# State scan of a hybrid decoder step: decays spread by DMA through DRAM, subtract and clip on ScalarE, output banks doubled

## What is computed

```python
def ssd_chunked(xs, dt, a, bm, cm, h0):
    xd = xs * dt[..., None]
    ad = dt * a
    def step(h, inp):
        xd_c, ad_c, b_c, c_c = inp
        acs = jnp.cumsum(ad_c, axis=1)
        seg = acs[:, :, None] - acs[:, None, :]
        lmat = jnp.exp(jnp.where(causal[None, :, :, None, None], seg, -jnp.inf))
        cb = jnp.einsum('blgn,bsgn->blsg', c_c, b_c)
        y_diag = jnp.einsum('blsg,blsgr,bsgrp->blgrp', cb, lmat, xd_c)
        y_off = jnp.einsum('blgn,bgrpn,blgr->blgrp', c_c, h, jnp.exp(acs))
        decay_end = jnp.exp(acs[:, -1:] - acs)
        h_new = h * jnp.exp(acs[:, -1])[..., None, None] + jnp.einsum('bsgn,bsgr,bsgrp->bgrpn', b_c, decay_end, xd_c)
        return h_new, y_diag + y_off
```

## Time and profile before

| what | value |
|---|---|
| median of 3 runs | 6118.93 us (6109.17 to 6125.71) |
| profiled execution | 6095.56 us, its span 6093.8 us |
| TensorE, VectorE, ScalarE, GpSimd busy | 4488.3, 3624.1, 1143.9, 2491.0 us |
| TensorE clock granted, mean | 0.864 |
| moved by DMA | 1467.90 MB, mean 241 GB/s |
| eight `ssd_chunk` stages | about 54 us (two) and 62 to 71 us (six) |

### The profile page before, as it was taken

One profiled execution on the slowest core, in us unless ns is written; L12 is line 12 of the kernel. 1 busy time (PEld: TensorE's weight loads), 2 busy tenths in 40 slices (PEclk: granted clock), 3 DMA queues, 4 the chain that ended last, 5 costly groups with the idle time before them and its releaser, 6 DMA issues. The chain is left out here.

```text
span 6093.8 us, 52161 instructions
## 1 busy us (share of the span) xinstructions
PE 4488.3 (74%) x16596; PEld 2712.1 (45%) x16596; DVE 3624.1 (59%) x8352; ACT 1143.9 (19%) x2862; POOL 2491.0 (41%) x2215
## 2 busy tenths in 40 slices
PE   6965982577878777469788777588777878547768
PEld 5344872453534555153444556273443566212223
DVE  4056437755656667676665767774566565854441
ACT  2022310111222111020222212111222201101111
POOL 0000010245433764436543444226433475377775
PEclk9965995788889988789898989799889989779999
DMA  3300740467565998679777976458666798599998
GB/s 128 112 17 19 260 146 0 158 232 258 180 213 183 381 336 302 205 269 373 264 234 247 390 271 227 130 181 306 206 205 202 266 394 315 187 351 409 395 377 306
DMA packets 574392, 1467.90 MB, mean 241 GB/s; under 512 B 59448, under 2 KB 250264, under 8 KB 567608
## 3 DMA queue, kind: packets, MB, share of 16 engines
q0 software_dynamic: 307200, 1115.82, 51.5%
q1 hardware_dynamic: 253960, 314.47, 15.3%
q10 hardware_dynamic: 12960, 34.26, 1.4%
HBM read 1418.60 MB, written 45.80 MB: 240 GB/s over the span
## 5 line engine op out<-in xcount | busy, mean ns | idle before, releaser
L2621 PE MATMUL bank<-vring,diag 128*128 128x512 f32 (+1 forms) x3064 | 1565.5, 649 | 474.7 <-ACT diag L2602 192.2
L2507 POOL DMA_INDIRECT uring<-in_peer_u,eidx x1024 | 1186.9, 1159 | 1227.3 <-DVE uring L2539 742.3
L2574 POOL DMA_INDIRECT vring<-in_peer_v,eidx x1024 | 1134.3, 1108 | 1336.7 <-PE bank L2621 935.1
L2539 DVE SCALAR_TENSOR_TENSOR uring<-uring,xr 128x1024 f32<-128x1024 f32 x1040 | 1263.9, 1222 | 585.2 <-DMA uring<-in_peer_u,eidx 540.0
L2621 PEld LDWEIGHTS bank<-vring,diag 128*128 128x128 f32 (+1 forms) x3064 | 572.8, 202 | 1279.7 <-issue 815.4
L634 PE MATMUL bank<-wt,xT 128*128 128x512 f32 (+3 forms) x1440 | 606.3, 580 | 90.1 <-DMA wt<-in_w_in 82.6
L2602 ACT ACTIVATE diag<-ident,wt 128x128 f32<-128x128 f32 x750 | 289.0, 398 | 1149.6 <-PE bank L2621 1034.1
L634 PEld LDWEIGHTS bank<-wt,xT 128*128 128x128 f32 (+1 forms) x1440 | 241.0, 178 | 444.1 <-issue 348.0
L2654 DVE SCALAR_TENSOR_TENSOR x_tok<-vring,wt,x_tok 128x1024 f32<-128x1024 f32 x274 | 356.7, 1302 | 90.8 <-DMA vring<-in_peer_v,eidx 76.8
L489 PE MATMUL bank<-xT,wx 128*128 128x264 f32 (+1 forms) x1536 | 371.6, 405 | 34.0 <-DMA wx<-in_w_in 33.8
L489 PEld LDWEIGHTS bank<-xT,wx 128*128 128x128 f32 x1536 | 307.7, 202 | 87.3 <-DMA wx<-in_w_in 34.1
(11 more groups left out here) (464 smaller groups left out, 5507.5 us busy)
## 6 DMA issues: line engine op xcount, KB each, us to landing
wt<-in_w_in SPq DMA_DIRECT2D x32, 2048.0 KB, 12.7
wx<-in_w_in SPq DMA_DIRECT2D x48, 1024.0 KB, 6.5
wm<-in_w_in SPq DMA_DIRECT2D x32, 1024.0 KB, 22.6
wm<-in_w_branch_a SPq DMA_DIRECT2D x32, 1024.0 KB, 15.4
wq<-in_peer_wq SPq DMA_DIRECT2D x32, 1024.0 KB, 9.0
tokm<-tout ACTq DMA_DIRECT2D x64, 256.0 KB, 4.6
s_h<-in_state_ssm SPq DMA_DIRECT2D x16, 1024.0 KB, 9.5
wm<-in_w_branch_b SPq DMA_DIRECT2D x16, 1024.0 KB, 13.4
```

What stands on the lines that cost most here:

```text
L2507: pool.indirect_dma_start(out=G.uring[:, K % UR, :], out_offset=None, in_=table, in_offset=bass.IndirectOffsetOnAxis(ap=E.tiles[q][3][:, j ...
L2539: dve.scalar_tensor_tensor(row, row, 1.0, G.xr[:, q % 2, :], ALU.mult, ALU.mult, accum_out=G.pre[:, q % 2, j:j + 1]).then_inc(G.dotted, 1)
L2574: pool.indirect_dma_start(out=G.vring[:, K % VR, :], out_offset=None, in_=table, in_offset=bass.IndirectOffsetOnAxis(ap=E.tiles[q][3][:, j ...
L2621: mm = pe.matmul(G.bank[6 + c][0:m, :], G.diag[:, R % DR, 0:m], G.vring[:, K % VR, c * BANK:(c + 1) * BANK], start=first, stop=last, skip_ ...
```

## The change

A DRAM tensor `decays` of 2x32x128 is added. SP writes `acsT` there, waits until it has landed, and reads it back four times, each time 8 rows (4 KB) broadcast to all 128 partitions, into three buffers of `eb` instead of two; the fourth waits for the first diagonal group. The spread matmuls are gone. ScalarE computes Relu(acs - spread value) for each head in place (8 instructions of 128x128 a group) and then Exp of the negative. VectorE has only the weighing, the masked product and the combine left; the masked product of the next group comes before the combine of this one. The diagonal part alternates between banks 0 and 1, the update of the state between 3 and 4, the part from the earlier state between 2 and 5, so L790 of a group waits for the combine two groups back. The copy of `acsT` comes first of the decay copies, and the mask product after them. The fractions at which expert slots are put into the order are shifted (`at`).

```diff
+EBR = 3
@@ ssd_chunk
-        eb, xdd, tmp = sb("eb", [P, 2, HPG * P]), S.xdd, S.ytmp
+        eb, xdd, tmp = sb("eb", [P, EBR, HPG * P]), S.xdd, S.ytmp
+        def at(g):
+            return 0.35 + 0.65 * max(0.0, g) / NG
@@ sync
             sp.dma_start(S.z[:], G.tokm[t * P:(t + 1) * P, 0:DI]).then_inc(sem("z"), 16)
+            sp.wait_ge(sem("acs"), 2)
+            sp.dma_start(G.decays[j], acsT[:]).then_inc(sem("kept"), 16)
+            sp.wait_ge(sem("kept"), 16)
+            for g in range(NG):
+                if g >= EBR:
+                    sp.wait_ge(sem("ydiag"), g - EBR + 1)
+                sp.dma_start(eb[:, g % EBR], G.decays[j, g * HPG:(g + 1) * HPG].rearrange("h l -> (h l)").partition_broadcast(P)
+                             ).then_inc(sem(f"spread{g % EBR}"), 16)
@@ scalar
             for g in range(NG):
-                go(0.25 + 0.75 * g / NG)
+                go(at(g - 0.8))
+                act.wait_ge(sem(f"spread{g % EBR}"), 16 * (g // EBR + 1))
+                for r in range(HPG):
+                    h = g * HPG + r
+                    e = eb[:, g % EBR, r * P:(r + 1) * P]
+                    act.activation(e, e, ACT.Relu, bias=acs[:, h:h + 1], scale=-1.0).then_inc(sem("seg"), 1)
                 act.wait_ge(sem("seg"), HPG * (g + 1))
-                act.activation(eb[:, g % 2], eb[:, g % 2], ACT.Exp).then_inc(sem("lmat"), 1)
+                act.activation(eb[:, g % EBR], eb[:, g % EBR], ACT.Exp, scale=-1.0).then_inc(sem("lmat"), 1)
@@ tensor
-            pe.wait_ge(sem("acs"), 3)
-            pe.wait_ge(sem("decays"), 3)
             pe.wait_ge(sem("xs"), 4)
-            def spread(g):
...
-            spread(0)
             for g in range(NG):
-                if g + 1 < NG:
-                    spread(g + 1)
-                go(0.25 + 0.75 * (g + 0.5) / NG)
-                if g == 0:
+                go(at(g - 0.1))
+                if g == 1:
                     pe.wait_ge(sem("cbm"), 1)
-                else:
-                    pe.wait_ge(sem("combined"), g)
-                pe.matmul(bank[5][:], cur[:, XT + NG + g, :], hT[:, g, :], start=True, stop=True)
+                    pe.wait_ge(sem("acs"), 3)
+                    pe.wait_ge(sem("decays"), 3)
+                elif g >= 2:
+                    pe.wait_ge(sem("combined"), g - 1)
+                pe.matmul(bank[(2, 5)[g % 2]][:], cur[:, XT + NG + g, :], hT[:, g, :], start=True, stop=True)
                 pe.wait_ge(sem("xdd"), g + 1)
-                pe.matmul(bank[3][:], btok[:, g, :], xdd[:, g % 2], start=True, stop=True)
+                pe.matmul(bank[3 + g % 2][:], btok[:, g, :], xdd[:, g % 2], start=True, stop=True)
+                go(at(g + 0.1))
                 pe.wait_ge(sem("mmat"), g + 1)
...
                 mm.then_inc(sem("ydiag"), 1)
-                go(0.25 + 0.75 * (g + 0.6) / NG)
+            go(0.95)
@@ vector
-            def prepare(g):
...
-                for r in range(HPG):
-                    h = g * HPG + r
-                    dve.tensor_scalar(eb[:, g % 2, r * P:(r + 1) * P], bank[r // 4][:, (r % 4) * P:(r % 4 + 1) * P],
-                                      acs[:, h:h + 1], 0.0, ALU.subtract, ALU.min).then_inc(sem("seg"), 1)
-            prepare(0)
+            weigh(0)
+            weigh(1)
+            masked(0)
             for g in range(NG):
+                if g + 1 < NG:
+                    go(at(g + 0.3))
+                    masked(g + 1)
+                go(at(g + 0.5))
...
                 dve.wait_ge(sem("ydiag"), g + 1)
...
+                if g + 2 < NG:
+                    weigh(g + 2)
+            dve.wait_ge(sem("combined"), NG)
@@ hybrid_step
+    G.decays = nc.dram_tensor("decays", (2, HS, P), F32, kind="Internal").ap()
```

More of the change, by code:

```diff
@@ L766, in _ @@
             go(0.25)
-            pe.wait_ge(sem("acs"), 3)
-            pe.wait_ge(sem("decays"), 3)
             pe.wait_ge(sem("xs"), 4)
-            def spread(g):
-                if g >= 1:
-                    pe.wait_ge(sem("seg"), HPG * g)
-                for r in range(HPG):
-                    h = g * HPG + r
-                    mm = pe.matmul(bank[r // 4][:, (r % 4) * P:(r % 4 + 1) * P],
-                                   G.ident[0:HS, h:h + 1].to_broadcast([HS, P]), acsT[:], start=True, stop=True)
-                mm.then_inc(sem("spread"), 1)
-            spread(0)
             for g in range(NG):
-                if g + 1 < NG:
-                    spread(g + 1)
-                go(0.25 + 0.75 * (g + 0.5) / NG)
-                if g == 0:
+                go(at(g - 0.1))
+                if g == 1:
                     pe.wait_ge(sem("cbm"), 1)
-                else:
-                    pe.wait_ge(sem("combined"), g)
-                pe.matmul(bank[5][:], cur[:, XT + NG + g, :], hT[:, g, :], start=True, stop=True)
+                    pe.wait_ge(sem("acs"), 3)
[3 more added lines that the diff above has]
+                pe.matmul(bank[(2, 5)[g % 2]][:], cur[:, XT + NG + g, :], hT[:, g, :], start=True, stop=True)
                 pe.wait_ge(sem("xdd"), g + 1)
-                pe.matmul(bank[3][:], btok[:, g, :], xdd[:, g % 2], start=True, stop=True)
+                pe.matmul(bank[3 + g % 2][:], btok[:, g, :], xdd[:, g % 2], start=True, stop=True)
+                go(at(g + 0.1))
                 pe.wait_ge(sem("mmat"), g + 1)
@@ L795, in _ @@
                     h = g * HPG + r
-                    mm = pe.matmul(bank[4][:, r * HPD:(r + 1) * HPD], eb[:, g % 2, r * P:(r + 1) * P],
+                    mm = pe.matmul(bank[g % 2][:, r * HPD:(r + 1) * HPD], eb[:, g % EBR, r * P:(r + 1) * P],
                                    xd[:, h * HPD:(h + 1) * HPD], start=True, stop=True)
                 mm.then_inc(sem("ydiag"), 1)
-                go(0.25 + 0.75 * (g + 0.6) / NG)
+            go(0.95)
         @block.vector
@@ L807, in _ @@
             go(0.15)
+            dve.wait_ge(sem("acsps"), 1)
+            a = Own(dve, sem("acs"))
+            a.mark(dve.tensor_copy(acsT[:], bank[4][0:HS, 2 * HS:2 * HS + P]))
+            a(dve.tensor_copy(acs[:], bank[4][:, 0:HS]))
+            a(dve.tensor_tensor(dec[:], bank[4][:, HS:2 * HS], acs[:], ALU.subtract))
             dve.wait_ge(sem("cb"), 1)
@@ L810, in _ @@
                               G.triu[:].unsqueeze(1).to_broadcast([P, NG, P]), ALU.mult).then_inc(sem("cbm"), 1)
-            dve.wait_ge(sem("acsps"), 1)
-            a = Own(dve, sem("acs"))
-            a(dve.tensor_copy(acs[:], bank[4][:, 0:HS]))
-            a.mark(dve.tensor_copy(acsT[:], bank[4][0:HS, 2 * HS:2 * HS + P]))
-            a(dve.tensor_tensor(dec[:], bank[4][:, HS:2 * HS], acs[:], ALU.subtract))
             dve.wait_ge(sem("xs"), 4)
@@ L822, in _, with weigh @@
             comb = Own(dve, sem("comb"))
-            def prepare(g):
-                hs = slice(g * HPG, (g + 1) * HPG)
+            def weigh(g):
                 dve.tensor_tensor(xdd[:, g % 2].rearrange("p (h d) -> p h d", h=HPG),
                                   xd[:, g * GW:(g + 1) * GW].rearrange("p (h d) -> p h d", h=HPG),
-                                  dec[:, hs].unsqueeze(2).to_broadcast([P, HPG, HPD]), ALU.mult).then_inc(sem("xdd"), 1)
-                dve.wait_ge(sem("spread"), g + 1)
-                for r in range(HPG):
-                    h = g * HPG + r
-                    dve.tensor_scalar(eb[:, g % 2, r * P:(r + 1) * P], bank[r // 4][:, (r % 4) * P:(r % 4 + 1) * P],
-                                      acs[:, h:h + 1], 0.0, ALU.subtract, ALU.min).then_inc(sem("seg"), 1)
@@ L837, in _, with masked @@
-            prepare(0)
+                                  dec[:, g * HPG:(g + 1) * HPG].unsqueeze(2).to_broadcast([P, HPG, HPD]), ALU.mult).then_inc(sem("xdd"), 1)
+            def masked(g):
+                dve.wait_ge(sem("lmat"), g + 1)
+                if g == 0:
+                    dve.wait_ge(sem("cbm"), 1)
+                m = eb[:, g % EBR].rearrange("p (h l) -> p h l", h=HPG)
+                dve.tensor_tensor(m, m, cbm[:, g, :].unsqueeze(1).to_broadcast([P, HPG, P]), ALU.mult).then_inc(sem("mmat"), 1)
```

21 lines of the change are left out of this document (8 added, 13 removed).

## The result

The changed kernel takes 6042.4 us (median of four runs, 6036.8 to 6049.5), the kernel before on the same chip 6117.3 (6109.2 to 6125.7): ratio 0.9874, 95% interval 0.9856 to 0.9892, or 75 us less. The prediction said 6070 us and 49 us less. The profiled execution after takes 6043.8 us, its span 6041.8.

A forecast was written before the change was run, and what follows sets the result against it. TensorE was taken to bound the six scan stages beside expert sums. Their 24 us and 25 us from the two bare stages made 49 us, taken from the median 6118.93 to give 6070 us; range 6034 to 6108.

The forecast's parts named there:

- rival A: Scan stages: TensorE keeps 2.4 GHz, gaining 45 us beside expert sums and 33 without, 78 us, to 6041 us; chance 0.2.
- bare stages: Scan stages 1 and 2, with no expert work beside them: 12.4 us gain a stage, 25 us for two.
- The bound in loaded stages: Six scan stages beside expert sums: TensorE bounds them, so work it loses is gain if the rest keeps it busy.
- T: End of a stage's first masked product, before which no diagonal matmul runs: 3.2 us earlier bare, unchanged loaded.
- The slow phase at T: Six stages beside expert sums: TensorE, idle some 5 us before T, then runs slow, costing about 3.5 us a stage.
- The size in loaded stages: Six stages beside expert sums: gain 3.4 us in two and 4.2 us in four, 24 us together, all after T.
- The chain: From acsT copied to T, through DRAM write, broadcast, Relu, Exp and product: 11.8 us bare, 14.8 us loaded.
- After T, bare: Stages 1 and 2: overlapped groups take 23.0 us instead of 32.2, the middle of 18.7 and 27.3; 9.2 us gain each.
- B: DMA chain late under gathers: T 5 us later in six stages eats 30 us, leaving 19 us gain, 6100 us; chance 0.17.
- C: TensorE stays at 1.2 GHz after T as expert slots starve between groups: 29 us slower, 6148 us; chance 0.08.
- D: Relu on ScalarE costs a table load, 1.28 us twice a group: gain about 29 us, 6090 us; chance 0.05.
- Hidden costs: Reordered masks (0.7 us a stage) hide behind the broadcast wait; the fourth broadcast, wanted some 10 us later, hides too.

The follow-up runs named there:

- the two repeats: The changed kernel, unchanged, timed and profiled again beside the kernel before in two later sets: 6005.0 us and 5995.0 us.
- The runs with one of the two put back: Changed kernel with single output banks and the earlier combine wait, 6037.1 us; or with spread matmuls back on TensorE, results unread, 6062.1 us.
- the run with the late chain: Changed kernel with two more writes of acsT to DRAM, each waited for, before the broadcasts: 6047.8 us, ratio 0.9956 to the kernel before.
- the unread spreads: Changed kernel with the 8 spread matmuls of each group back on TensorE, their output overwritten unread: 6062.1 us, ratio 0.9983 to the kernel before.

## Why the prediction was right, and where it was off

**The forecast and its band.** The time, 6042.4 us, is inside 6034 to 6108, but the gain of 75 us is outside the 35 to 65 that I gave 0.5. What holds the time inside is the reach into rival A, whose 78 us and 6041 us are nearly what was measured, and A's reason holds in the bare stages only. That the range still covered the total is in part luck.

**The bound in loaded stages: right.** TensorE works after T without a wait, and what left it is a gain: with the spreads back in, 51 us are lost. The slow phase at T was put at 3.5 us; stage 6 shows 3.3. From T to TensorE's last matmul 31.6 us were forecast for stage 3; the four stages of that kind have 31.9, 31.6, 31.9 and 31.4.

**The size in loaded stages: off, 24 forecast, 40 measured.** Three terms. (1) After T, 30.2 us instead of 23.6. In stages 5 and 6 I left 11 slots behind T by the new places in the order, and there are 10 (40 records of L2626), 2 x 1.77 = 3.5 us. In the other four the gain up to TensorE's last matmul is 16.6 us, as forecast (16.8), but I had measured to that matmul and not to the end of the stage. In stages 4 and 8 of before the stage ended 2.1 and 1.8 us after it, and now it ends 0.4 us after it; that makes the other 3 us. Before, a last expert dot on VectorE ended after that matmul (1665.8 against 1665.2 in stage 4), and a gather was issued behind it; that this is what held the end back is read from the timeline and not tested. (2) acsT to T, forecast level, is 4.0 us shorter: the forecast 14.8 us a stage is 14.1 measured. (3) Start to acsT, which the change hardly touches, is 5.6 us shorter on the first chip but only 1.4 (82.0 to 80.6) on the second. In that pair the loaded stages gain 37.0 instead of 40.0, so some of the 40 is spread between executions.

**The chain: right in form, and the miss is nearly all in one link, the write.** Bare, forecast and measured: SP's wake-up 0.5 and 0.41, write and wait 2.5 and 1.40, broadcast 3.9 and 3.98, Relu 2.5 and 2.48 to the start of Exp, Exp 1.2 and 1.08, product 1.2 and 1.23; sum 11.8 and 10.6 us. g2row was the right row for the broadcast. For the write I had no row of its kind and went above the nearer one of 1.8 us; even that was too long. (That row, gate_s<-gsmp, isn't a write to DRAM at all, both tiles lie in SBUF.) Loaded, write and wait are 1.4 to 4.3 us, mean 2.9 (forecast 3.5), and the broadcast 4.7 to 8.2, mean 6.0 (5.9). The Trainium skill ("DMA: Bandwidth & Descriptors", Anatomy of one DMA — SWDGE (gpsimd) path) gives a transfer that GpSimd issues a fixed cost of about 2.0 us, mostly the receipt of the write. This write is issued by SP, and with 1.40 us from one issue to the next in a quiet stage it stays below that figure.

**After T, bare: the mechanism right, the size off, and this is the worst term.** I worked out 18.7 us for 2.4 GHz and 27.3 for 1.2 and took the middle, 23.0; it is 17.9 in both stages, and 18.6 to 19.4 in the two repeats: the high end. The middle was no likely value: TensorE is granted 1.2 or 2.4 GHz, and I should have asked what separates the two cases. Before, it stops for the combine in stage 1 twice (0.73 and 2.70 us) and also for the masked product; take the stops and the spreads away, and after one slow group it stays at 2.4 GHz until its last diagonal group. The runs with one of the two put back (0.66 and 0.65 in stage 1) show that the change needed both. After T is 11 of the 13 us missing in bare stages; the shorter write makes most of the rest.

**The rivals.** A (TensorE keeps 2.4 GHz, 78 us less) came out half: its bare 33 us were 37.7, and its sum is near the measured 75. But its reason fails in loaded stages: in the first profile the first diagonal group takes 3.67 or 3.68 us in all six. In the repeats one stage each is free of it (2.00 us, in stage 4 after a stop of 2.96 us and in stage 8 after one of 2.42). B (chain late): the run with the late chain shows its price to be the one put on it, but T was not late. In that run T came 7.4 us later a stage and cost 7.2. C (TensorE slow after T) didn't occur: granted clock 0.81 to 0.94 in loaded stages, and no wait after T. The waits that go with a slow TensorE in the bare stages of before are for VectorE and not for DMA, and the run with the unread spreads is slow with no wait after T at all, so this case doesn't show C's mechanism in the bare stages either. D (a table load for Relu) didn't occur.

**Hidden costs: right.** The mask (L817) and the weighing end at 331.3 in stage 1, 4.4 us before the first product. The fourth broadcast, which waits for a diagonal group, delays nothing on the path: its Relu starts at 344.44 and the product that needs it at 348.45, with VectorE busy in between.

**What the medians hid.** I set the 49 us against the median and not against the profiled execution, which was right: the profiled execution of before is 22 us under its median, that of after is at its median, and between the two lies a last stretch that is 39 us longer, which the repeat didn't show again.

## What to carry to other kernels

Find the one event that splits a stage into work that can't wait for it and work that must, and price what comes before it one to one, even where the bounding engine looks full. A copy through DRAM takes work off a full engine, but its latency (from the issue of the write to the first use 5.4 us in stage 1 and 6 to 12 us beside gathers) belongs behind that event: let the engine do the first group itself and the DMA the rest. Where two clocks are possible, don't forecast the mean of them; ask which waits stand between the groups, and expect that removing one of two causes gives less than half of the gain.

## What the runs showed of the hardware

- A 16 KB write to DRAM followed by a wait costs SP 1.40 us from issue to next issue in a quiet stage, and 1.4 to 4.7 us beside gathers at 236 to 273 GB/s. From the issue of the broadcasts (4 KB rows to 128 partitions) to the first Relu it is 3.8 to 4.3 us quiet and 4.4 to 8.2 us beside gathers (both from three profiles of the changed kernel).
- Eight tensor_scalar of 128x128 in 32 bits take 1.65 us from SBUF and 2.16 from a bank, 0.21 and 0.27 us each. The Trainium skill ("VectorE: DVE Perf Modes", Why PSUM operands drop a tier) says that a bank operand costs such an operation its double rate in 32 bits; the trace agrees in direction, a quarter less and not half, for rows of 128 elements.
- In bare stage 1 TensorE, never idle after T with the unread spreads in, did its groups at 1.2 GHz until 353 us, 18 us after T; in the changed kernel, after a stop of 4.18 us and with fewer matmuls, it was at 2.4 GHz from 343 us on, 6 us after T. That it is kept busy doesn't tell these two cases apart, and what does stays open.
- The last stretch of this kernel, with the same code, took 746 to 761 us in twelve profiled executions and 799 in one.
